# Weights' rounded values and remainders side by side, moved operand read backwards, in a two-model float32 kernel

## What is computed

```python
h = h + 0.5 * swiglu_ffn(rms_norm(h), w_gate_up, w_down)          # 1024 -> 2 x 2816 -> 1024
u = rms_norm(h)
q, k, v, ca, cg = split(u @ w_in)
h = h + concat(norm(window_attention(q, k, v)), norm(conv31(ca, cg))) @ w_out
h = h + 0.5 * swiglu_ffn(rms_norm(h), w_gate_up2, w_down2)
h = h + sigmoid(h @ w_ple_gate) * rms_norm(p @ w_ple)
```

## Time and profile before

| | us |
|---|---|
| median of the timed runs (2) | 3952.62 |
| lowest, highest | 3951.73, 3953.51 |
| span of the profiled execution, first to last instruction | 3950.6 |
| PE busy in it | 3812.4 |
| DVE busy | 2334.5 |
| ACT busy | 1510.9 |
| POOL busy | 511.5 |

### The profile page before, as it was taken

The page is one execution under the profiler, slowest core; times in us unless marked ns, Lnnn a source line. Parts: engine busy times, 40 slices in busy tenths (PEclk is TensorE's granted clock), DMA queues, the critical chain, the costliest instruction groups (busy, mean ns, idle before and its releaser), DMA issues. The chain is left out here.

```text
span 3950.6 us, 46607 instructions
## 1 busy us (share of the span) xinstructions
PE 3812.4 (97%) x17790; PEld 3050.4 (77%) x17790; DVE 2334.5 (59%) x3213; ACT 1510.9 (38%) x2188; POOL 511.5 (13%) x366
## 2 busy tenths in 40 slices
PE   8999989999999998999989999999999999999997
PEld 6888758888788885788877678788877767878886
DVE  5455766445544475744467675775567665675656
ACT  3224653223322365322243444343343353343333
POOL 1001731000100055100020013200010002220002
PEclk9999989999999999999999999999999999999999
DMA  4333203333233330233332100122233110022222
GB/s 152 96 96 112 66 21 96 96 96 111 86 98 99 97 106 11 79 100 96 96 114 80 49 22 1 43 96 96 96 109 107 59 38 6 12 80 96 96 96 80
DMA packets 87018, 314.99 MB, mean 80 GB/s; under 512 B 10016, under 2 KB 10400, under 8 KB 86176
## 3 DMA queue, kind: packets, MB, share of 16 engines
q1 hardware_dynamic: 83664, 302.43, 24.4%
q10 hardware_dynamic: 3152, 9.74, 0.7%
HBM read 307.94 MB, written 2.10 MB: 78 GB/s over the span
## 5 line engine op out<-in xcount | busy, mean ns | idle before, releaser
L384 ACT ACTIVATE wh<-raw 128x1024 fp32r<-128x1024 f32 x564 | 597.4, 1059 | 1630.3 <-PE ps L404 1317.5
L402 PE MATMUL ps<-xh,wh 128*128 128x512 f32 x2336 | 918.0, 393 | 16.7 <-DVE xl L467 10.0
L403 PE MATMUL ps<-xl,wh 128*128 128x512 f32 x2336 | 910.8, 390 | 0.0
L404 PE MATMUL ps<-xh,wl 128*128 128x512 f32 x2336 | 910.5, 390 | 0.0
L388 DVE TENSOR_TENSOR wl<-raw,wh 128x1024 fp32r<-128x1024 f32 x564 | 695.6, 1233 | 181.1 <-ACT wh L384 180.2
L402 PEld LDWEIGHTS ps<-xh,wh 128*128 128x128 f32 x2336 | 439.8, 188 | 112.4 <-issue 19.6
L403 PEld LDWEIGHTS ps<-xl,wh 128*128 128x128 f32 x2336 | 440.0, 188 | 94.3 <-issue 3.6
L404 PEld LDWEIGHTS ps<-xh,wl 128*128 128x128 f32 x2336 | 439.8, 188 | 91.9
L402 PE MATMUL ps<-fh,wh 128*128 128x512 f32 x1016 | 397.1, 391 | 4.0 <-DVE wl L388 4.0
L404 PE MATMUL ps<-fh,wl 128*128 128x512 f32 x1016 | 395.4, 389 | 0.0
L403 PE MATMUL ps<-fl,wh 128*128 128x512 f32 x1016 | 395.3, 389 | 0.0
(11 more groups left out here) (467 smaller groups left out, 5529.6 us busy)
## 6 DMA issues: line engine op xcount, KB each, us to landing
raw<-in_w SPq DMA_DIRECT2D x564, 512.0 KB, 3.5
con<-in_consts SPq DMA_DIRECT2D x1, 2053.5 KB, 14.0
h<-in_x SPq DMA_DIRECT2D x4, 512.0 KB, 6.9
p_t<-in_p ACTq DMA_DIRECT2D x4, 512.0 KB, 3.9
w1k<-in_w1c ACTq DMA_DIRECT2D x2, 1024.0 KB, 4.9
w1v<-in_w1c ACTq DMA_DIRECT2D x2, 1024.0 KB, 7.0
out<-h SPq DMA_DIRECT2D x8, 256.0 KB, 2.2
dup_k<-roped ACTq DMA_DIRECT2D x8, 128.0 KB, 3.6
```

What stands on the lines that cost most here:

```text
L384: nc.scalar.activation(wh[k % 2][:, :], raw[k % 4][:, :], ACT.Copy).then_inc(s["w_hi"], 1)
L402: nc.tensor.matmul(DB[k % 2][:, :], a, hi(q), start=(q == order[0]), stop=False)
L403: nc.tensor.matmul(DB[k % 2][:, :], a, lo(q), start=False, stop=False)
L404: last = nc.tensor.matmul(DB[k % 2][:, :], b, hi(q), start=False, stop=(q == order[-1]))
```

## The change

- **Weights.** In place of wh[2] and wl[2], each two buffers of 128 x 1024, there are two buffers of 128 x 1024 x 2: element [x, 0] is the rounded value of weight x, [x, 1] its remainder. w_hi(k) and w_lo(k) are views with a step of 8 B. ACT writes the one, DVE reads it and writes the other, PE loads 128 weights from either with that step.
- **Moved operand.** along(k, ap) turns a 512-column view round: pe_unit and pe_chunks read the moved tile from its last column to its first, and write the PSUM row in the same reversed order, so that what lies where in PSUM stays as it was. The two PLE loops take the new weights but are not turned.
- **Six stretches.** HALVES lists for each of six stretches of units an offset in bytes and whether the moved operand is reversed: (0, yes), (64, yes), (0, no), (32, yes), (128, yes), (192, yes). The weights' buffers of a stretch start (512 - offset) % 512 B into a region that is 512 B longer than they are. Stretches 1 and 2 are the first model's first layer, split before unit 82, stretches 3 and 4 its second layer split alike (units 168 to 249 and 250 to 335), 5 and 6 the second model's layers (336 to 449, 450 to 563).
- **Layout.** fh and fl start 256 B later than before, relative to xh and xl, so a stretch has one distance for x tiles and another, 256 B further, for f tiles. w0 and w1 take the place of wh and wl behind raw. The DMA scratch that the program reserves shrinks to 4,096 B, which moves all tiles 12,288 B down, and con and everything behind it by another 256 B modulo 512. With offset 0 the weights start 256 B (modulo 512) from the x tiles and at the f tiles' offset.
- **Order.** No instruction is added, removed or moved on any engine: PE, DVE, ACT, POOL and SP have the same rows in the same order.

```diff
         xl = sb("xl", [P, DC, T], F32R)
+        sb.at += LINE // 2
         f_at = sb.at
...
-        wh = [sb(f"wh{k}", [P, UW], F32R) for k in range(2)]
-        wl = [sb(f"wl{k}", [P, UW], F32R) for k in range(2)]
+        w_at = [sb.at, sb.at + 8 * UW + LINE]
+        sb.at += 2 * (8 * UW + LINE)
...
+        HALVES = [(0, True), (64, True), (0, False), (32, True), (128, True), (192, True)]
+        SETS = len(HALVES)
+        pairs = [[Layout(nc, w_at[k] + (LINE - HALVES[n][0]) % LINE, 8 * UW)(f"w{k}_{n}", [P, UW, 2], F32R)
+                  for k in range(2)] for n in range(SETS)]
+
+        def set_of(k):
+
+            i = max(n for n in range(len(blocks)) if at_unit[n] <= k)
+            if blocks[i][0] == 2:
+                return 4 + blocks[i][1]
+            return 2 * blocks[i][1] + (k - at_unit[i] >= U1_PLE)
+
+        def w_hi(k, x=0, y=UW):
+            return pairs[set_of(k)][k % 2][:, x:y, 0]
+
+        def w_lo(k, x=0, y=UW):
+            return pairs[set_of(k)][k % 2][:, x:y, 1]
+
+        def along(k, ap):
+
+            return ap[:, ::-1] if HALVES[set_of(k)][1] else ap
...
-            nc.scalar.activation(wh[k % 2][:, :], raw[k % 4][:, :], ACT.Copy).then_inc(s["w_hi"], 1)
+            nc.scalar.activation(w_hi(i * 4 + k), raw[k % 4][:, :], ACT.Copy).then_inc(s["w_hi"], 1)
...
-            nc.vector.tensor_tensor(wl[k % 2][:, :], raw[k % 4][:, :], wh[k % 2][:, :].bitcast(F32),
+            nc.vector.tensor_tensor(w_lo(i * 4 + k), raw[k % 4][:, :], w_hi(i * 4 + k).bitcast(F32),
                                     ALU.subtract).then_inc(s["w_lo"], 1)
...
-                a, b = wh[k % 2][:, q * P:(q + 1) * P], wl[k % 2][:, q * P:(q + 1) * P]
-                nc.tensor.matmul(DB[k % 2][:, :], a, hi(q), start=(q == order[0]), stop=False)
-                nc.tensor.matmul(DB[k % 2][:, :], a, lo(q), start=False, stop=False)
-                last = nc.tensor.matmul(DB[k % 2][:, :], b, hi(q), start=False, stop=(q == order[-1]))
+                u = i * 4 + k
+                a, b = tile_of(u, q)
+                row = along(u, DB[k % 2][:, :])
+                nc.tensor.matmul(row, a, along(u, hi(q)), start=(q == order[0]), stop=False)
+                nc.tensor.matmul(row, a, along(u, lo(q)), start=False, stop=False)
+                last = nc.tensor.matmul(row, b, along(u, hi(q)), start=False, stop=(q == order[-1]))
```

More of the change, by code:

```diff
@@ L28 @@
 UW = DC * P
+LINE = 512
 FFN_UNITS = sum(2 * g + DC for g in GROUPS)
@@ L229, in stream, with tile_of @@
             return io[f"w{blocks[i][0]}"][blocks[i][1]]
+        HALVES = [(0, True), (64, True), (0, False), (32, True), (128, True), (192, True)]
[13 more added lines that the diff above has]
+            return ap[:, ::-1] if HALVES[set_of(k)][1] else ap
+        def tile_of(k, q):
+            return w_hi(k, q * P, (q + 1) * P), w_lo(k, q * P, (q + 1) * P)
         def start_block(first, sems):
@@ L410, in pe_chunks @@
             for n, q in enumerate(chunks):
[L411 to L414, removed]
+                a, b = tile_of(k, q)
+                row = along(k, DB[k % 2][:, :])
+                nc.tensor.matmul(row, a, along(k, hi(q)), start=start and n == 0, stop=False)
+                nc.tensor.matmul(row, a, along(k, lo(q)), start=False, stop=False)
+                last = nc.tensor.matmul(row, b, along(k, hi(q)), start=False, stop=stop and n == len(chunks) - 1)
             return last
@@ L806, in ple @@
                                     col = (n % 4 * 2 + q) * P
-                                    w_h, w_l = wh[u % 2][:, col:col + P], wl[u % 2][:, col:col + P]
+                                    w_h, w_l = tile_of(u, col // P)
                                     mm(BK[4][:, :], w_h, p_hi[:, q, :], start=(q == 0), stop=False)
@@ L2587, in _ @@
                                         pe.wait_ge(s["x_lo"], q + 1)
-                                    ins = pe_chunks(n, x_hi, x_lo, (q,), q == 0, q == DC - 1)
+                                    ins = pe_chunks(o + n, x_hi, x_lo, (q,), q == 0, q == DC - 1)
                                     if n == 0 and q == 4 and joined:
@@ L3056 @@
     from concourse.bass_utils import run_bass_kernel_spmd as _run
-    nc = _bacc.Bacc("TRN2", target_bir_lowering=False, num_devices=1)
+    nc = _bacc.Bacc("TRN2", target_bir_lowering=False, num_devices=1, dynamic_dma_scratch_size=4096)
     arrays = {"in_" + k: v for k, v in layout(inputs, WHICH).items()}
```

## The result

The changed kernel takes 4035.18 us (median of two runs, 4032.87 and 4037.48) against 3952.62 before: ratio 1.0206, 95% interval 1.0189 to 1.0222. The profiled execution took 4032.87 us, its span is 4031.1 us, 80.5 more than before.

What follows compares the result with a forecast made beforehand. PE bounds the kernel, through the distance between matmul starts. Gains of 113.6, 5.1 and 9.0 us make 127.7; less 8 for waits, 120 us off 3952.6 gives 3832 us, 8-in-10 range 3790 to 4025.

Steps and rivals of the forecast that it cites:

- the rule of two independent ports: Trainium skill's rule that loading the next weights takes nothing from PE's running matmul; kept under no change, chance 0.19.
- 13.4 and 20 ns: Excess per 512-column matmul over the clock's 213.3 ns: first value at 226.7 ns, second at the gates' 233.3.
- The failed step: Weight matmuls outside PLE and the third stretch, 11,136, fall from 226.7 to 216.5 ns start to start: 113.6 us gained.
- The gates: The gates' 768 matmuls start from 233.3 ns, so they gain 6.6 ns each on top: 5.1 us more.
- The third stretch: Units 168 to 249, read forwards: 1,920 matmuls at 222 ns, 9.0 us gained; standing apart would tell the load's direction.
- x and f units were to differ: Sign: if distance decides, x and f units within one stretch, 256 B apart, should differ too; no size given.
- no change: Rival: excess no layout touches, or stretches gaining 10 ns while others lose as much; 3952 us, chance 0.19.
- Waits (8 us off): In attention, mixers, w_in and PLE, PE waits for DVE and ACT, so shorter matmuls buy less: 8 us off.
- the splits (0): ACT's and DVE's writes of weights 8 B apart cost 0; bound 48 us; as a rival 4000 us, chance 0.04.
- PSUM reversed (0): Matmul output rows written backwards in PSUM cost 0; bound a loss up to 253 ns per matmul.
- the scratch (0): Smaller DMA scratch moves all tiles by 12,288 B, a multiple of 512: 0.
- The slower one: Rival: spread weights or wrong direction make matmuls 240 ns, 4129 us; at 233 ns 87 us lost, 4040; chance 0.15.

Runs made afterwards that it cites:

- experiment 1: Changed kernel with weights packed again (4 B apart) and the moved operand read forwards, at six distances between weights and moved tiles; 3999.08 us (before 3952.42).
- experiments 3 and 4: Unreversed with weights 8 B apart: changed kernel read forwards at six distances, 4032.10 us; six further distances, 4025.74 us. The second number also has packed runs, 4002.11 and 4047.81.
- experiment 6: Kernel before plus smaller DMA scratch and one half of the change: reversal alone 4039.23 us (1.0211), weights 8 B apart alone 4033.35 us (1.0195).
- experiment 5: Packed weights at distance 0, with moved read and PSUM write reversed together, each alone, or neither, by stretch; 4012.80 us (before 3956.76).
- experiment 8: Kernel before with gates' tiles at distance 0 and smaller DMA scratch, 1.0028; smaller scratch alone, 1.0008; gates' tiles moved 128 B, old scratch, 1.0016.

## Why the prediction was wrong

**Bound: right.** PE's distance from start to start decides: the account above finds 76 of 80.5 us there.

**Layout matters, against the rule of two independent ports: right.** Shown by experiment 1. The prediction read 13.4 and 20 ns as two values of one thing that depends on distance; they are that, but the values are several; 233.3 is the most common, and 226.7 the best, at two of the sixteen distances that x tiles or gates had with packed weights and an unreversed read. That the kernel before stood at one of the two for x and f tiles was luck. The trace already held the warning: 233.3 at two distances that are 256 B apart, 226.7 at one. The prediction used it only as an upper bound.

**The failed step:** "I take 216.5, next to the earlier trace rows, because with equal speeds there is no drift to make them meet again." It was to give 113.6 us. Of the same 11,136 matmuls the 768 of the gates stayed at 233.3 ns and the other 10,368 went there from 226.7, a loss of 10,368 x 6.6 = 68.4 us; the third stretch adds 1,920 x 6.6 = 12.7, together 81 us by these rows. (The account above has 76 for the same thing, from the trace's averages.) The distance was 233.3 ns in the changed kernel at five distances modulo 256 (0, 64, 128, 192, 224), and in the runs apart never below 230.0 with spread weights or 233.3 with a reversed read. The earlier trace rows is a row of another kind of matmul, with columns at half the rate, where the excess is all but absent; it bore on the question whether 215 is possible, not on whether this edit gets there. The argument needed three things that no row showed: that the load takes the weights from the last to the first, that a spread load runs at the moved operand's full speed, and that the excess consists of meetings that can be lined up away. Whichever way the load goes, either the reversed read of the changed kernel or the unreversed one of experiments 3 and 4 goes the same way, and neither came under 230.0; so the order of the load is not what was missing. The load's record did not get longer in proportion to the memory passed over, 195 ns against 188, so the second may well hold. The third is what fell: at distance 0 an excess of the same size at 320 and at 512 columns, and one that grows with fewer weights, does not look like a count of meetings along the way. What it is instead is not settled by these runs.

**The gates** were to give 5.1 us more; they stood at 233.3 and still do: 0. **The third stretch** was to be at 222 and to tell the direction by being apart: 233.3 like the rest. It tells nothing, since spread weights cost the same unreversed at distance 0 (experiment 6).

**x and f units were to differ** if the distance decides. They do not, since the 256 B between them are one whole period: for the same reason the change's shift of fh and fl does nothing. The bet under "no change" that some stretches gain as others lose had the right cause but not the outcome: from one of the best places there was nothing to gain.

**Waits (8 us off), the splits (0), PSUM reversed (0), the scratch (0):** the first had nothing to apply to, as no time was gained. The splits cost nothing on the path, as said, though ACT's is 115 ns longer, where a dense write of DVE had been the row. PSUM is 226.8 against 226.7 ns (experiment 5), the scratch 1.0008 with an interval that holds 1 (experiment 8).

**The rivals.** The slower one gave the price of the case that came: at 233 ns a loss of 87 us, 4040 us; 4035.18 was measured. Its mechanism was only half right. It had the cost go with the memory passed over, 240 ns at the old distance and more at others; each of the edits costs 6.6 ns at distance 0, whatever memory is passed over (the reversal passes over no more than before), and together no more than alone. That the time came within 5 us of its price is because it had been worked out for 233 ns, the gates' value, and not because of its mechanism. It had a chance of 0.15, and the range ended below it at 4025. It would have been given more weight by asking what any of the three edits does to a pair of operands that already has the better of two observed values.

## What to carry to other kernels

Where a stream of matmuls shows two distances from start to start for the same instruction, find out first which operand places have the better one, by a run with several placements in one program, before giving up that placement for an argument about how the reads meet. When one layout has the better value, price every edit that leaves it at the other value seen in the trace, once for all edits together, and not at zero. And a gain of a few us in one stretch is worth nothing until the granted clock of the other stretches has been compared: here the moved gates gave 4.8 us, and more was lost at half clock.

## What the runs showed of the hardware that was not expected

- With 128 weights and 512 moved columns of float32r a matmul takes 226.7 ns when the weights' and the moved tile's addresses agree modulo 256 B, 226.9 when the weights start 120 B behind (one gate, 189 distances), and 228.3 to 234.3 at the fourteen other distances seen. The good places are narrow: 4 B from 0 it is 232.4, 8 B from 120 it is 233.3.
- A moved operand read backwards gives 233.3 to 236.6 ns at each distance tried; the PSUM row written backwards costs nothing (226.8).
- Weights 8 B apart give 230.0 to 233.4 ns with the moved operand read forwards, and a load record of 195 ns against 188.
- At distance 0 the excess over the columns' own time is 13.5, 13.5 and 13.6 ns for 512, 384 and 320 columns, 16.0 for 448; with 80 weights per load in place of 128 it rises to 20.0. At half clock it is absent (425 ns for 512 columns).
- ACT writes 1024 elements 8 B apart in 1174 ns against 1059 side by side; DVE's subtraction, which reads and writes at that step, stays at 1237 against 1233.
- With the gates' tiles moved, the same instructions in the same order ran longer at half clock elsewhere: a mixer's window had clock 0.69 or 0.66 in place of 1.00. In another execution of the second of these kernels that window had 1.00, so the layout alone does not decide it.
